# A second probability tile in four rounds of each layer is turned in blocks by VectorE and brought over by four transfers that GpSimd issues

## The reference, cut to what matters

```python
def win_attention(q, k, v):                       # the selected branch: the same, on ks and vs
    s = einsum('bnqkgd,bnpkd->bnkgqp', qb, kw) * SCALE
    p = softmax(where(mask, s, NEG))
    return einsum('bnkgqp,bnpkd->bnqkgd', p, vw)
...
o_cmp, p_cmp = cmp_attention(q, kc, vc)           # 31 compressed keys
gates = sigmoid(gate_logits)
y_nsa = gates[0] * o_cmp + gates[1] * o_slc + gates[2] * o_win
y = concatenate([y_lru * silu(g_lru), y_nsa * silu(g_nsa)])
return x + y @ w_out
```

## Time and profile before

| | us |
|---|---|
| runs | 544.32, 539.6, 543.06 (median 543.06) |
| profiled execution | 540.08 |
| its span | 538.3 |
| granted TensorE clock in it, share of full | 0.999 |
| PE busy | 523.8 (97%) |
| DVE busy | 379.9 (71%) |
| ACT busy | 309.9 (58%) |
| POOL busy | 46.8 (9%) |

### The profile page before, as it was taken

The page is one execution under the profiler, slowest core; times in us unless marked ns, Lnnn a source line. Parts: engine busy times, 40 slices in busy tenths (PEclk is TensorE's granted clock), DMA queues, the critical chain, the costliest instruction groups (busy, mean ns, idle before and its releaser), DMA issues.

```text
span 538.3 us, 8590 instructions
## 1 busy us (share of the span) xinstructions
PE 523.8 (97%) x3095; PEld 395.6 (73%) x3095; DVE 379.9 (71%) x620; ACT 309.9 (58%) x625; POOL 46.8 (9%) x88
## 2 busy tenths in 40 slices
PE   8999999999899999999999999999989999999995
PEld 7777868778677766767887687678777777676784
DVE  3596996679857686855747589668986768678432
ACT  5757735624766666663534772653475656667523
POOL 4101100130000000000520110012100000000000
PEclk9999999999999999999999999999999999999999
DMA  9876464365222222321323845635523232111013
GB/s 263 203 226 185 97 180 103 73 149 126 76 74 65 56 55 69 79 58 40 90 90 98 213 124 142 119 94 119 136 62 96 61 97 52 50 38 34 8 41 117
DMA packets 102426, 54.65 MB, mean 102 GB/s; under 512 B 42080, under 2 KB 100592, under 8 KB 102384
## 3 DMA queue, kind: packets, MB, share of 16 engines
q1 hardware_dynamic: 99232, 49.63, 36.1%
q0 software_dynamic: 1536, 3.15, 2.4%
q10 hardware_dynamic: 1616, 1.32, 0.8%
HBM read 44.12 MB, written 2.10 MB: 86 GB/s over the span
## 4 chain that ended last, share of the span: by engine, by line
PE 67%; DVE 16%; issue 5%; SPq 4%; ACT 3%; DMA 3%; POOL 1%; POOLq 0%; DVEq 0%; ACTq 0%
PE z_ps L1634 10%; PE z_ps L1636 10%; PE z_ps L1635 10%; PE o_ps L1775 5%; PE t_ps L1737 5%; PE a_ps L1775 4%; PE s_ps L1714 3%; DVE w_lo L1233 3%; PE z_ps L1714 3%; PE o_ps L1634 3%; PE o_ps L1636 2%; PE o_ps L1635 2%; ACT probs L1160 2%; DMA swp<-E 2%; DVE E L1282 2%
## 5 line engine op out<-in xcount | busy, mean ns | idle before, releaser
L1634 PE MATMUL z_ps<-h_hi,w_hi 128*128 128x512 f32 x248 | 101.5, 409 | 4.3 <-DVE E L1282 4.2
L1636 PE MATMUL z_ps<-h_hi,w_lo 128*128 128x512 f32 x248 | 97.0, 391 | 0.0
L1635 PE MATMUL z_ps<-h_lo,w_hi 128*128 128x512 f32 x248 | 96.8, 390 | 0.0
L982 ACT ACTIVATE w_hi<-stage 128x1024 fp32r<-128x1024 f32 x54 | 57.1, 1058 | 53.9 <-PE z_ps L1636 29.1
L1233 DVE TENSOR_TENSOR w_lo<-stage,w_hi 128x1024 fp32r<-128x1024 f32 x54 | 65.9, 1220 | 8.6 <-ACT w_hi L982 7.9
L1169 ACT ACTIVATE probsT<-t_ps 128x512 f32<-128x512 f32 (+1 forms) x70 | 41.7, 595 | 43.8 <-PE t_ps L1737 34.1
L1634 PEld LDWEIGHTS z_ps<-h_hi,w_hi 128*128 128x128 f32 x248 | 46.6, 188 | 18.7 <-issue 8.2
L1636 PEld LDWEIGHTS z_ps<-h_hi,w_lo 128*128 128x128 f32 x248 | 46.5, 188 | 10.3
L1635 PEld LDWEIGHTS z_ps<-h_lo,w_hi 128*128 128x128 f32 x248 | 46.7, 188 | 8.3 <-issue 0.2
L1522 DVE TENSOR_REDUCE mn<-s_ps 128x1 f32<-128x384 f32 (+3 forms) x44 | 26.2, 637 | 32.4 <-PE s_ps L1722 32.3
L1160 ACT ACTIVATE probs<-s_ps,mn 128x128 f32<-128x128 f32 (+3 forms) x64 | 33.1, 527 | 16.4 <-DVE mn L1522 16.2
(11 more groups left out here) (266 smaller groups left out, 1052.7 us busy)
## 6 DMA issues: line engine op xcount, KB each, us to landing
stage<-in_w_in SPq DMA_DIRECT2D x27, 512.0 KB, 4.1
stage<-in_w_in SPq DMA_DIRECT2D x34, 256.0 KB, 3.9
probsT<-swp SPq DMA_DIRECT2D x72, 64.0 KB, 2.1
stage<-in_cmp_k_w SPq DMA_DIRECT2D x8, 512.0 KB, 4.0
stage<-in_cmp_v_w SPq DMA_DIRECT2D x8, 512.0 KB, 4.5
stage<-in_w_out SPq DMA_DIRECT2D x8, 512.0 KB, 3.3
stage<-in_w_out SPq DMA_DIRECT2D x16, 256.0 KB, 3.7
swp<-E POOLq DMA_DIRECT2D x48, 64.0 KB, 2.3
```

Source lines behind the costliest of these rows:

```text
L982: act.activation(split_into(n)[0], stage_of(key), ACT.Copy).then_inc(hi_split, 1)
L1634: pe.matmul(bank, w_hi[:, slot, at:at + P], x_hi, start=first, stop=False)
L1635: pe.matmul(bank, w_hi[:, slot, at:at + P], x_lo, start=False, stop=False)
L1636: ins = pe.matmul(bank, w_lo[:, slot, at:at + P], x_hi, start=False, stop=last)
```

## The change

In sets 4, 6, 8 and 10 of both layers, the last tile of the set is far too (`SECOND_FAR`: P2001, P2101, P3002 and P3102 in the names that leave out the layer, read as query block, branch, pair, key block). In sets 4 and 6 the C tile moves ahead of that tile. The second far tile's D stands right behind the first one's, a round ahead. Its transfers are issued by POOL, each queue has a semaphore of its own, and `far` numbers count both kinds, so that which of the two `swp` buffers a tile takes, and which earlier transfers its D waits for, change too. Eight tiles are moved in all: 32 PE transposes and 8 ACT copies go, 8 STREAM_TRANSPOSE and 32 transfers come.

```diff
-    sets += [[*unit(2, b, pair), c[2 * (2 + b) + pair]] for b in range(2) for pair in range(2)]
+    sets += [[*unit(2, b, pair)[:2 + pair], c[2 * (2 + b) + pair], *unit(2, b, pair)[2 + pair:]] for b in range(2) for pair in range(2)]
...
-FAR = {tiles[0] for tiles in SETS[2:-1]}
+SECOND_FAR = {SETS[n][-1] for n in (4, 6, 8, 10)}
+FAR = {tiles[0] for tiles in SETS[2:-1]} | SECOND_FAR
...
-                if n < len(SETS) and SETS[n][0] in FAR:
-                    add(("D", SETS[n][0]))
+                if n < len(SETS):
+                    add(*(("D", key) for key in SETS[n] if key in FAR))
...
-        if n < len(SETS) and SETS[n][0] in FAR:
-            add(("DX", SETS[n][0]))
+        if n < len(SETS):
+            add(*(("DX", key) for key in SETS[n] if key in FAR))
...
-        blocks_ok, landed = sem("blocks_ok"), sem("landed")
+        blocks_ok, landed = sem("blocks_ok"), [sem("landed_sp"), sem("landed_pool")]
...
-            eng.wait_ge(landed, 64 * (f + 1))
+            second = plan.far[f][1:] in SECOND_FAR
+            eng.wait_ge(landed[second], 64 * sum((key[1:] in SECOND_FAR) == second for key in plan.far[:f + 1]))
...
+        def bring(eng, key):
+
+            f = far_no[key]
+            eng.wait_ge(blocks_ok, f + 1)
+            wait_slot(eng, key)
+            for a in range(4):
+                eng.dma_start(slot_of(key)[:, a * P:(a + 1) * P],
+                              swp[32 * a:32 * a + 32, f % N_SWP, :].rearrange("b (c n) -> b c n", c=4)).then_inc(landed[key[1:] in SECOND_FAR], 16)
...
-                elif kind == "DX":
...
+                elif kind == "DX" and st[2] not in SECOND_FAR:
+                    bring(sync, (st[1], *st[2]))
...
+                elif kind == "DX" and st[2] in SECOND_FAR:
+                    bring(pool, (st[1], *st[2]))
```

## The result

| | before | changed |
|---|---|---|
| median of 20 runs, us | 540.95 | 544.54 |
| lowest and highest, us | 539.6, 544.32 | 542.78, 546.65 |
| profiled execution, us | 540.08 | 546.5 |
| its span, us | 538.3 | 544.8 |

The ratio of the changed kernel to the kernel before is 1.0058, 95% interval 1.0042 to 1.0074: 3.1 us slower. The forecast was 541.5 us, with a range of its own from 539 to 544, and 0.3 us to be saved. The measured 544.54 us lies just outside that range. It is within 1% of the kernel before and inside the range for 8 in 10, but the change is clear of noise and goes the other way. The base was not the trouble: the 541.8 us taken for the kernel before is 0.9 us above the median of its twenty runs, so the error of the change itself is larger than that of the time.

What follows compares the result with a forecast made beforehand. PE was taken as the bound, busy 523.8 of 538.3 us. Gains less new DVE waits saved 0.7 us, less 0.4 for W left 0.3: 541.8 - 0.3 = 541.5 us, range 539 to 544, 8 in 10 537.5 to 546.5.

Steps and rivals of the forecast that it cites:

- It has nothing else in the attention, so its own time costs nothing: POOL issuing four transfers a tile in the attention: its own time put at nothing, only the last landing counts.
- TensorE's gain, 0.44 us a tile: Four PE transposes saved per second far tile: 0.44 us each, 3.5 us at most for eight tiles.
- The switches of W: C tile between 128-key tiles in sets 4 and 6: one more switch back, 0.1 us four times, 0.4 us.
- The path: Second D delays minima, exponentials, ACT's copy of turned coefficients, then PE's next-round first turn; slacks 0.75, 0.59, 0.45 us.
- DVE's delays, layer 0: PE's waits from the second D in layer 0: 0.71, 0.10 and 0.70 us, 1.51 lost against 1.32 saved.
- the lag of DVE in round 4 and the tanh: Layer 0, round 5: DVE not following PE's 0.44 us lead, plus 0.25 us for the tanh behind the C tile's copy.
- the grown wait for the coefficients: Layer 0, round 10: PE's existing wait for DVE's coefficients moves back by 0.70 us; its saved turn gains nothing.
- DVE's delays, layer 1: PE's waits from the second D in rounds 5, 7, 9 of layer 1: 0.88 us lost against 1.76 saved.
- I put it at nothing, up to 0.5 us a round: First far tile's D waiting for the previous round's transfers in rounds 5, 7, 9: nothing, at most 0.5 us a round.
- POOL's landing: Four transfers land 4.3 us after issue may begin; tightest in layer 0's round 10, with 5.3 us available.
- the third rival: POOL's issue grows with pieces, transfers land late, W waits: 560 us, or near 546 at 1.6 us an issue; chance 0.12.
- the rival in which DVE becomes the bound: No slack covers the second D, 1.04 us in each of six rounds: 3.8 us slower, 545.6 us; chance 0.12.

Runs made afterwards that it cites:

- e2: The kernel before, plus 32 small transfers by GpSimd (128 rows of 32 bytes each) that nobody waits for: 544.72 us, ratio 1.0055.
- e3: The kernel before, plus 32 small transfers by GpSimd (16 rows of 32 bytes each) that nobody waits for: 544.18 us, ratio 1.0042.
- e4: The changed kernel without the second far tiles' block transposes and transfers, their products using what lies in the slot: 539.12 us, ratio 0.9953.
- e6: The changed kernel with SP issuing all second-tile transfers and a third buffer (rstd) for second tiles of sets 6, 8, 10: 541.12 us, ratio 0.9989.
- e8: Against the kernel before: second far tiles in sets 4, 6, 8 only, old W order, later block transposes, third buffer, SP issuing: 539.35 us, ratio 0.9956.
- e1: The changed kernel, but SP also issues the second far tiles' transfers, behind those of the first: 541.76 us, ratio 1.001.

## Why the prediction was wrong, point by point

- **The missing term.** The step that failed is "It has nothing else in the attention, so its own time costs nothing". The transfers were costed by issue, by landing and by who waits for them, and POOL's own time was put at nothing. A transfer issued by GpSimd leaves 82 ns of drain behind for the end of the program, 2.6 us for 32, and this is three quarters of the 3.5 us that the traces account for. No rival had it. The trace before showed where to look: its last computing row ends at 534.85 and its span is 538.3, and the records have GpSimd's DRAIN of 4.6 us ending last, so that whatever lengthens it lengthens the program. The price of a transfer in it took e2 and e3.
- **TensorE's gain, 0.44 us a tile:** right (0.44 to 0.48 in e4), but for round 10 of layer 0, where no gain was forecast. The switches of W were put at 0.1 us and cost 0.15. That PE stands without a gap in the attention but for one place is a misreading: the kernel before waits 2.12 us for DVE at the start of each attention, the place behind which the clock falls.
- **The path.** The prediction followed the second D through the minima, the exponentials and the copy of the coefficients to the first turn of the next round. That path is there: in layer 1 PE waited 0.22 and 0.36 us at the first turns of rounds 8 and 10, for 0.27 and 0.59 forecast, in layer 0 under 0.1. The path that it lacked goes from D by Y, YH and the copy of a turned tile to T(B) in the same round, and on it PE lost more, 0.33 and 0.66 us in layer 1.
- **DVE's delays, layer 0.** Round 5: forecast 0.71, 0.20 came, by T(B); the lag of DVE in round 4 and the tanh, 0.69 of it, did not add up as I had it. Round 7: 0.10, and nothing came. Rounds 9 and 10: 0.70 for the grown wait for the coefficients, and 0.55 came (its row grew from 0.37 to 1.19; without the second D, in e4, it is 0.81, since PE is 0.44 early). The mechanism was right, and that set 10's turn would give nothing.
- **DVE's delays, layer 1.** Forecast 0.02, 0.27 and 0.59; in the changed kernel rounds 5, 7 and 9 lost 0.40, 0.18 and 0.73 against e4, and rounds 8 and 10 did not keep all of their 0.44 either. Here "I put it at nothing, up to 0.5 us a round" for the landings failed: e6 shows that 1.15 us of layer 1's loss with SP was this wait, most of it on the second block transpose.
- **POOL's landing** in the tightest place, round 10 of layer 0: the prediction had 5.3 us for 4.3, and 0.65 us were missing. In the trace the previous W ends at 235.43, the issue begins at 236.00, the fourth issue at 237.58, and it lands at 241.65: 6.2 us. The 2.3 us for the landing was the median of transfers ahead of the attention, and this one took 4.1 beside a load of weights. So W did wait for POOL's transfers, the sign named for the third rival, and yet that rival is wrong: an issue took 0.57 us, with four times the pieces of one that took 0.50. (Its "near 546" does not add up either: 541.8 + 9.6 - 3.5 is 547.9.)
- **The sum of the attention** was forecast at -0.3 us and is +0.88 as changed, -0.14 with SP as the issuer. That the second is near is luck. By layer the forecast was +0.39 and -0.68, and with SP it was -0.30 and +0.16. The measured 544.54 lies near the 545.6 of the rival in which DVE becomes the bound, and that is luck too, since most of the loss is the drain.
- **Rule and row.** What the prediction set against the rows from the Trainium skill ("VectorE: DVE Perf Modes", "Rules for kernel authors": TensorE for a 128x128 transpose) holds in one place and not in another. The runs decide by the idle time: e8 shows DVE's way winning 0.47 us a tile where DVE has room, e1 shows it winning nothing where it hasn't.

## What to carry to other kernels

The price of a transfer has a part that no row of its own place shows: look at what the program does between its last computing row and the end of its span, and for whom it waits there. Transfers issued by GpSimd are paid once more in its next drain, by their number; issue them from another queue, or drain where GpSimd is idle. When work moves from the busiest engine to one with 71% busy time, what counts is the idle time on every path from the moved work to an instruction of the busiest engine, also by a third engine that runs in order, and a second tile in flight wants a buffer of its own.

## What the runs showed of the hardware that was not expected

- GpSimd's DRAIN: 0.65 us with no transfer since the last one, 4.59 with 48, 6.61 (no instruction ahead of it) and 7.20 to 7.21 (one ahead) with 80. Rows of 32 bytes or 512, 16 or 128 of them, make no difference.
- The queue of GpSimd's transfers counts 32 packets for each transfer in every kernel here (1536 for 48, 2560 for 80), whatever its rows.
- 64 KB transfers of GpSimd that landed in 2.0 to 2.5 us in layer 1 took 3.5 to 4.9 us in layer 0 when a load of weights had been issued just ahead of them.
- Identical stretches of two programs (e2, e3 and the kernel before) keep the same offset to 0.03 us over 100 us, but two executions of the changed rounds of layer 1 differ by 0.47 us where block transposes wait for landings. The clock's fall behind a 2.1 us idle time of PE at the start of the attention comes in some executions and not in others, 3.4 us at 1.2 GHz, 1.6 us of time.
